# Three weight strips computed together at the start of three phases

## The reference

```python
# first block, end of layer 0 and start of layer 1
h = h + gate * (p[i] @ w_ple_proj[i])
hk = rmsnorm(h, kv_norm)                  # keys and values of the shared attention
k_shared = partial_rope((hk @ w_k)..., pos); v_shared = (hk @ w_v)...
q = rmsnorm(h, norm_mix[1]) @ w_q
...
# second block, layer 0: its input is rmsnorm(first block, norm_final)
u = rms_norm(h, pre_norm[0]); q, k, v, g_ret, cb, cc, cx, g_conv = split_cols(u @ w_in, ...)
h = h + rms_norm(y, post_norm[0])         # after the output projection "eout"
# second block, layer 1: latent attention
cq, ckv, k_rope, gate = split_cols(rms_norm(h, pre_norm[1]) @ w_in, ODD_SPLITS)
q = rms_norm(cq, q_a_norm) @ w_qb; kv = rms_norm(ckv, kv_a_norm) @ w_kvb
```

## Time and profile before

| | |
|---|---|
| median of 3 runs | 2060.14 us (2056.61 to 2063.57) |
| profiled execution: time, span | 2060.03 us, 2057.5 us |
| TensorE busy | 1959.6 us |
| VectorE, ScalarE, GpSimd busy | 934.9, 747.6, 880.1 us |
| granted TensorE clock, mean | 0.952 of full speed |

### The profile page before, as it was taken

How to read it: one execution, slowest core, us unless ns; L and a number is a source line. 1 busy time by engine, 2 the same in 40 slices (tenths; PEclk the granted TensorE clock), 3 DMA queues, 4 the chain that set the end, 5 groups by cost and what they waited for, 6 DMA issues and landing times.

```text
span 2057.5 us, 25021 instructions
## 1 busy us (share of the span) xinstructions
PE 1959.6 (95%) x8728; PEld 1577.0 (77%) x8728; DVE 934.9 (45%) x1444; ACT 747.6 (36%) x1172; POOL 880.1 (43%) x1159
## 2 busy tenths in 40 slices
PE   2999999999999899999999999899999999899996
PEld 1888888888888666688888888787887878586674
DVE  7995232121226578642221215742255551556554
ACT  7223333232324445534332324422233342333561
POOL 1042555555555511245555555554444445262221
PEclk8556999999999999999999999999999999899998
DMA  3245333333333300123323332232222223131111
GB/s 136 52 129 151 105 95 99 102 92 92 102 92 92 111 30 31 32 85 109 97 97 95 95 97 84 82 101 82 86 78 82 74 79 96 60 111 46 42 41 41
DMA packets 59296, 175.24 MB, mean 85 GB/s; under 512 B 14784, under 2 KB 15168, under 8 KB 58560
## 3 DMA queue, kind: packets, MB, share of 16 engines
q1 hardware_dynamic: 57344, 170.34, 27.5%
q10 hardware_dynamic: 1872, 3.80, 0.6%
HBM read 163.37 MB, written 4.19 MB: 81 GB/s over the span
## 4 chain that ended last, share of the span: by engine, by line
PE 85%; DVE 9%; ACT 3%; issue 1%; DMA 1%; SPq 0%; DVEq 0%; ACTq 0%
PE ps L799 24%; PE ps L801 23%; PE ps L800 23%; PE ps L860 1%; PE ps L862 1%; PE ps L958 1%; PE ps L977 1%; PE ps L1131 1%; PE ps L929 1%; PE ps L925 1%; PE ps L1130 1%; PE ps L1140 1%; PE ps L914 1%; DVE rstd L1361 1%; DVE h L1481 1%
## 5 line engine op out<-in xcount | busy, mean ns | idle before, releaser
L424 POOL TENSOR_TENSOR wlo<-raw,whi 128x256 fp32r<-128x256 f32 x1152 | 869.8, 787 | 1135.1 <-ACT whi L455 1135.1
L455 ACT ACTIVATE whi<-raw 128x1024 fp32r<-128x1024 f32 x288 | 302.1, 1052 | 394.1 <-PE ps L801 386.8
L799 PE MATMUL ps<-Ch,whi 128*128 128x512 f32 x912 | 364.8, 400 | 5.5 <-DVE Cl L1345 5.4
L801 PE MATMUL ps<-Ch,wlo 128*128 128x512 f32 x912 | 356.5, 391 | 0.0
L800 PE MATMUL ps<-Cl,whi 128*128 128x512 f32 x912 | 356.3, 391 | 0.0
L799 PE MATMUL ps<-Ah,whi 128*128 128x512 f32 x656 | 265.8, 405 | 15.0 <-DVE Al L1345 11.5
L801 PE MATMUL ps<-Ah,wlo 128*128 128x512 f32 x656 | 257.1, 392 | 0.0
L800 PE MATMUL ps<-Al,whi 128*128 128x512 f32 x656 | 256.8, 391 | 0.0
L799 PE MATMUL ps<-Bh,whi 128*128 128x512 f32 x640 | 250.9, 392 | 0.0
L801 PE MATMUL ps<-Bh,wlo 128*128 128x512 f32 x640 | 249.3, 390 | 0.0
L800 PE MATMUL ps<-Bl,whi 128*128 128x512 f32 x640 | 249.2, 389 | 0.0
(11 more groups left out here) (330 smaller groups left out, 2300.5 us busy)
## 6 DMA issues: line engine op xcount, KB each, us to landing
raw<-in_w SPq DMA_DIRECT2D x288, 512.0 KB, 3.6
u<-in_xch SPq DMA_DIRECT2D x1, 2048.0 KB, 11.8
yg<-vsb SPq DMA_DIRECT2D x16, 128.0 KB, 2.3
yg<-z SPq DMA_DIRECT2D x16, 128.0 KB, 2.3
ysc<-yg ACTq DMA_DIRECT2D x8, 256.0 KB, 2.0
h<-in_xfm SPq DMA_DIRECT2D x2, 1024.0 KB, 6.2
out<-h SPq DMA_DIRECT2D x8, 256.0 KB, 2.0
bB<-in_bc SPq DMA_DIRECT2D x1, 1024.0 KB, 7.3
```

The lines of the kernel that those rows point to most:

```text
L424: last = nc.gpsimd.tensor_tensor(wlo[:, r, cc], raw[:, r, cc], whi[:, r, cc].bitcast(F32), ALU.subtract)
L455: nc.scalar.activation(whi[:, slot, :], raw[:, slot, :], ACT.Copy).then_inc(hi_ready, 1)
L799: nc.tensor.matmul(out, whi[:, slot, w], xh, start=first, stop=False)
L801: return nc.tensor.matmul(out, wlo[:, slot, w], xh, start=False, stop=last)
```

## The change

At the start of kv, even and odd, TensorE computes the first three strips together: it takes input tile k, makes its products with strips 0, 1 and 2 into three banks, and goes on to tile k + 1. The norms that stood behind strip 0 (kv), behind strip 1 (even) and inside strip 0 (odd, the squares) now end behind the group of three; the partner product of odd stands behind strip 3 instead of strip 1. On ScalarE `ahead(kv, 0)` goes in front of the root, and `ahead(odd, 0)` in front of the eight high parts of the latents' input.

```diff
             act.dma_start(msk1[:, :, :], a["msk1"]).then_inc(in_a1, 16)
+            ahead("kv", 0)
             root(D)
-            for l in range(NSTR["kv"]):
+            for l in range(1, NSTR["kv"]):
                 ahead("kv", l)
...
             act.dma_start(cm[:, :], a["cm"]).then_inc(in_cm, 16)
+            ahead("odd", 0)
             for m in range(KT):
                 asked()
                 high("A", m, h[:, m, :], gain("pre1", m))
...
             root(D)
             O0 = OUT0["odd"]
-            ahead("odd", 0)
...
+            def first_strips(name, x, xt, step=1, each=None):
+
+                pe.wait_ge(lo_ready, S0[name] + LEAD)
+                pe.wait_ge(evac, OUT0[name] + LEAD - RING)
+                for k in range(KT):
+                    pe.wait_ge(x_lo, xt + step * k + 1)
+                    for l in range(LEAD):
+                        last = product((S0[name] + l) % RING, k, (OUT0[name] + l) % RING, X[x][0][:, k, :], X[x][1][:, k, :], k == 0, k == KT - 1)
+                        if k == KT - 1:
+                            last.then_inc(seg_done, 1)
+                    if each is not None:
+                        each(k)
...
-            strips("kv", "A", XT["kvq"], 2, n=NSTR["kv"], between=norm)
+            first_strips("kv", "A", XT["kvq"], 2)
+            norm()
+            strip("kv", 3, 3, "A", XT["kvq"], 2)
...
-            for l in range(8):
+            first_strips("even", "C", XT["even"])
+            norm()
+            norm(acc2, SX)
+            for l in range(LEAD, 8):
                 even(l)
-                if l == 1:
-                    norm()
-                    norm(acc2, SX)
...
-            for l in range(NSTR["odd"]):
-                strip("odd", l, l, "A", XT["odd"], each=None if l else add_squares)
-                if l == 1:
+            first_strips("odd", "A", XT["odd"], each=add_squares)
+            for l in range(LEAD, NSTR["odd"]):
+                strip("odd", l, l, "A", XT["odd"])
+                if l == LEAD:
                     pe.wait_ge(evac, OUT0["odd"] + 1)
                     partners(18, "perm2", kr[:, :], SX)
                 if l == 4:
```

## The result

The changed kernel takes 2076.88 us (median of 4 runs, 2075.14 to 2077.82), the kernel before in the same rounds 2061.53 us. The ratio is 1.0077, 95% interval 1.0057 to 1.0097: 15 us slower, clear of the 0.3% that the text ahead sets. The forecast was 2078.1 us in a range of 2068 to 2083. The profiled execution has a span of 2072.7 us, 15.2 us more than the one before.

What follows compares the result with a forecast made beforehand. TensorE, busy 95% of the span, was taken to bound the kernel. Keys -2.1 + L, second block +4.45 + 2L and latents +6.1 + L gave 8.45 + 4L = +18.1 us, so 2078.1 us; own range 2073.5 to 2081.5, with rivals 2068 to 2083.

Steps and rivals of the forecast that it cites:

- L: Time lost to the low clock behind each of four new idle stretches of TensorE: 2.4 us, bounds 1.5 and 2.85.
- keys, whole stage: Keys: late group start, three strips at 16.32 us, then norm and one more strip; -2.1 + L = +0.3 us.
- second block, whole stage: Second block's input: idle before the group and again before strip 4, clock low behind both; +4.45 + 2L = +9.3 us.
- latents, whole stage: Latents: query latents' norm starts later, TensorE idle 6 us before it, clock low behind; +6.1 + L = +8.5 us.
- The weights' wait: Keys and second block: group waits for the third strip's low part from GpSimd, TensorE idle 4.9 and 6.3 us.
- VectorE's chain of 18.8 us: Latents: VectorE's work on outputs 1 to 3 after the last squares product, holding the query latents' norm; 18.8 us.
- the norm one strip too late: Second block: only strip 3 now covers the norm's chain, so TensorE waits 5.6 us in front of strip 4.
- Moved at no cost: Keys and latents: issuing `ahead(kv, 0)` and `ahead(odd, 0)` earlier, one ScalarE activation of 1.05 us each, costs nothing.
- the third strip's weights are in time: Rival, keys and second block: idle 4.9 and 6.3 us nearly vanish; -2.8 + 2L = +2.0, 2062.0 us; chance 6%.
- The covered norm: Rival, latents: shorter VectorE work covers the query latents' norm; -6.1 - L, 2069.6 us; chance 7%.
- the held clock: Rival, new idle gaps: clock stays up, 4L less, 2068.5 us; in one or two gaps 2073 to 2076; chance 9%.
- The rule on banks: Rival, all three groups: changing banks drops the clock to 1.2 GHz, some 53 us more, 2127 us; chance 2%.

Runs made afterwards that it cites:

- filler: Changed kernel with thrown-away products put into its four idle stretches of TensorE; 2067.78 us, ratio 1.0039 to the kernel before.
- early_split: Changed kernel with ScalarE issuing the splits of the last gate iterations up to one output earlier in both gate phases; 2064.1 us, ratio 1.0026 to the kernel before.
- late_rotation: Changed kernel with VectorE's rotation of the rope key moved behind output 3's square and low part; ratio 1.0068 to the kernel before.
- pair: Kernel before with two strips together, six tiles each first, at keys and second block only, ahead("kv", 0) before the root; 2047.57 us, ratio 0.9934.
- only_second: Kernel before with the group of three at the second block's input alone; 2069.26 us, ratio 1.0042.
- only_keys: Kernel before with the group of three at the keys alone; 2059.25 us, ratio 0.9991.
- only_latents: Kernel before with the group of three at the latents alone; 2067.43 us, ratio 1.0037.
- pair_filler: pair with 33 thrown-away products behind eout's norm product, in front of the latents; 2046.62 us, ratio 0.9937 to the kernel before.
- late_norm: Changed kernel with the norm of the query latents moved from in front of strip 5 to behind it; ratio 1.0090 to the kernel before.

## Why the prediction was right

Stage by stage, with L as the loss of the clock:

| term | forecast | measured |
|---|---|---|
| keys: idle in front of the group | 4.9 | 4.74 |
| keys, whole stage | -2.1 + L = +0.3 | +0.9 in the trace, -1.0 timed alone |
| second block: idle in front | 6.3 | 6.19 |
| second block: idle in front of strip 4 | 5.6 | 5.76 |
| second block, whole stage | +4.45 + 2L = +9.3 | +9.0, and +9.0 timed alone |
| latents: last squares product to norm | 18.8 | 18.98 |
| latents, whole stage | +6.1 + L = +8.5 | +7.4 in the trace, +7.2 timed alone |
| L, four times | 9.6 | 9.9 in the trace, 8.9 by the filler |
| sum | +18.1 | +15.4 by the medians, +15.2 in the trace |

**Right, and shown.** The weights' wait, by early_split, which took away 8.1 of the 10.9 us of waiting for GpSimd and left the other two waits as they were. VectorE's chain of 18.8 us, by late_rotation. The clock, by filler. **Right, and shown by the trace alone:** the norm one strip too late. Its wait is 5.76 us, and the distance from norm to strip 4 is 13.1 us where it was 12.97. pair, with this norm where it was, has 1.07 us of waiting left there; but no run moves this norm by itself. The trace's four L: keys 3.0 (681.10 + 16.32 = 697.42, norm at 700.43), second block 2.5 (1310.18 + 16.32 = 1326.5, norm at 1329.00) and 2.0 (from that norm to the evacuation of strip 4, 20.7 us against 18.7), latents 2.4 (from their norm to the next phase's first product, 8.7 against 6.3).

**Off in size.** The latents' term was 1.1 us too large: I put the last squares product 25.6 us behind the first tile, it was 24.5 (1782.49 to 1806.96). The low clock at the start of the group ended after 3.9 us, before it had lasted 5.65. The forecast took over the loss of the execution before, which is chance. So is the good fit at the keys in the table: the four other executions with this code took 35.5 to 35.7 us, 0.4 us less than the kernel before and not 0.9 more, and their L there is nearer 1.6 than 3.0. "Moved at no cost" was 0.2 us off: with `ahead("odd", 0)` moved, the first input tile of the latents comes 7.23 to 7.25 us behind the start of VectorE's reciprocal in all seven kernels that have it there; in the four that do not, and have nothing filled in there, it is 7.06 us.

**Not foreseen.** The stage between keys and second block, identical in all kernels here, took from 590.6 to 596.2 us. In the kernel before, attention ran in part at the low clock (0.89 in a window at 730 to 745 us, 0.94 at 830 to 860), in the changed kernel at 1.00, and in only_second at 0.77 in the second of them. That is 2.5 us in favour of the changed kernel in the two profiled executions, and with the 0.7 us ahead of the keys the distance between 18.3 (all other stages) and 15.2. All other eleven executions took 592.1 us or more there, so the changed kernel's 590.6 is a lucky one. In the profiled execution the luck there and the long stage at the keys partly cancel. The ratio is known to about 4 us either way, so the measured total by itself cannot tell the forecast's 18.1 from 15.4; the stages and the waits carry the account.

Of the 1.0 us in front of the latents 0.2 are the moved split; the rest is eout's norm, whose two products ran in part at the low clock (TensorE, before and after):

```profile
1765.79 1.14 PE L914 MATMUL ps<-acc,cst 128*128 128x512 f32 x2 [2.17 <-DVE acc L1355]
```

```profile
1772.54 1.96 PE L928 MATMUL ps<-acc,cst 128*128 128x512 f32 x2 [2.17 <-DVE acc L1372]
```

It comes again in other runs. In the six executions with the group of three at the second block and nothing filled in, VectorE's reciprocal starts 2.4 to 2.8 us behind this norm product, and in the three kernels without that group (before, only_keys, only_latents) and in filler 1.9 us; pair and pair_filler lie between, at 2.3 and 2.4. The wait in front of it is 2.17 us in all of them. Why the clock falls earlier in some stays open; so does whether attention meets the low clock less often in the changed kernel.

**The rivals.** The one by which the third strip's weights are in time is what early_split nearly made: 0.26% or 5.4 us above the kernel before, where the rival gave +2.0 with no wait left at all (its interval, 3.3 to 7.6 us, stays above that). The covered norm and the held clock did not come by themselves. The rule on banks (the Trainium skill, TensorE: Matmul & The Clock Gate, "A second HAM failure mode: psum-queue depth-cycling") had 2%. That page of the Trainium skill tells of a kernel that cycles through banks, in which TensorE's short idle moments between groups of matmuls let the clock swing between its levels; 2127 us, with all three groups low throughout, was a bound above that. No run here has such swings: with 72 matmuls that change the bank every third, the clock stayed at 1.00 in filler's windows, and from 687.48 to 700.43 the changed kernel has 0.227 us a matmul and no idle moment between them. So the trace does not show that changing banks alone costs clock.

## What to carry to other kernels

Taking several weight strips per input tile removes the wait for late tiles, but it asks at the start for what used to be wanted a strip or two later (here the third strip's split), and it moves every result behind the group to its end: check the readiness of the last strip, and the length of each chain that the removed strips used to cover. Use just as many strips as are ready and as the late tile needs, and work on the tiles that exist first: two strips with six tiles each in hand, at two places, gave 12.7 us where three from the first tile on, at three places, cost 15. And when a wait is moved, read the queue of every engine that waits for what stands behind it; late_norm moved one wait of 6.1 us and got two others, of 1.4 and 2.8 us, with the clock low behind the second.

## What the runs showed of the hardware that was not expected

**VectorE beside GpSimd.** In the changed kernel GpSimd has five low parts in a row behind the group of the keys, and one multiplication of VectorE with both inputs in SBUF, 0.69 us in the kernel before (at 712.94), took 4.57 us. VectorE's and GpSimd's timelines:

```profile
712.47 0.69 DVE L1383 TENSOR_TENSOR q<-ps,rstd 128x512 f32<-128x512 f32 x1 [4.17 <-PE ps L802]
713.19 4.57 DVE L1386 TENSOR_TENSOR ev<-kv,rope 128x512 f32<-128x512 f32 x1
717.69 0.68 DVE L1388 TENSOR_TENSOR ev<-ps,rope 128x512 f32<-128x512 f32 x1
```

```profile
703.20 14.01 POOL L424 TENSOR_TENSOR wlo<-raw,whi 128x256 fp32r<-128x256 f32 x20 [12.33 <-ACT whi L455]
```

It ended 0.55 us after GpSimd's last subtraction, and so it did in all seven profiled executions with the group of three at the keys (4.56 to 4.65 us): it lay beside six subtractions, which kept their usual 0.75 us each, and finished only when all were done. Where the two meet elsewhere such an operation takes 1.1 to 1.2 us, and the subtractions beside it 1.2; what makes the difference stays open. The Trainium skill, GPSIMD Engine Reference, section "Specifications", says that the two share their interfaces to SBUF and that VectorE's instructions with two SBUF inputs contend; these rows agree and give a size. TensorE did not wait for it.

**A low clock is not always a loss.** The same fall of the clock cost 2 to 3 us behind each new wait, where TensorE set the pace, and nothing that can be measured at the first tiles of the latents (pair_filler against pair), where VectorE did.

**The clock held over some short waits, and not over others.** In early_split it stayed at 1.00 over waits of 0.90 and 1.91 us, in late_norm over 1.42. In the changed kernel it fell over 4.74 us and more, but in late_norm also over 2.82 (0.50 from 1841.05 to 1844.44), and around the 2.17 us in front of eout's norm it was 0.54 in the changed kernel (1772.54 to 1774.50) and 0.94 in the kernel before (1765.79 to 1766.90). No single length of a wait can be read from these runs.
